# A transformer block on one core: the remainder of the expert weights formed by two engines, or by one

## The chip, the cores and the metric

The kernel runs on one core of one Trainium2 chip. The time is device microseconds (us) of one execution, the median of several. Lower is better. Five engines run side by side and meet only at semaphores: PE (TensorE, matrix products), DVE (VectorE), ACT (ScalarE), POOL (GpSimd) and SP (SyncE, which here only issues DMAs).

## The reference, cut to what matters

One layer: modulation, attention of two kinds, an output projection, and then a mixture of experts over 1024 tokens. Only the experts matter here, since the change lies wholly in them. Each token goes to 4 of 32 experts:

```
for each block of at most 128 tokens of one expert e:
    hu  = x @ w1[e] + b1[e]                       # 1024 -> 2048
    glu = min(hu[:, 0::2], 7); lin = clip(hu[:, 1::2], -7, 7)
    act = glu * sigmoid(1.702 * glu) * (lin + 1)  # 1024
    y   = act @ w2[e] + b2[e]                     # 1024 -> 1024
```

## The kernel before

The products are kept close to float32 by splitting both operands: a value is written as hi, its rounding to the fast float32 format (fp32r), and lo, the remainder. A product is then three passes: hi times hi, hi times lo of the weights, lo times hi.

**Steps.** A step is one expert with R = 1 or 2 blocks of 128 tokens. The loop of `program` runs a single step (R = 1) and then a double one (R = 2), over and over, and ends with single steps alone. In this run there are 35 steps: 16 pairs of a single and a double step, and 3 single steps at the end, so 19 single and 16 double ones.

**Units.** A step needs six weight units of 2 MB, each 128 partitions x 8 slices (k) x 512 columns: units 0 to 3 of w1 (`UP`), 4 and 5 of w2 (`DOWN`). For each unit and block PE does `product`: 8 slices x 3 passes = 24 matmuls. What happens to a unit n:
- SP loads it into a ring of three buffers, `ring[n % 3]` (L1163). The buffer becomes free when unit n - 3 has been split, so the load waits for `lo_done` (L1160, DVE's part) and `pool_lo_done` (L1161, POOL's part) of that unit.
- ACT writes `w_hi`, a ring of three, in two halves of four slices (L1256).
- The remainder `w_lo = ring - w_hi`, a ring of two, is formed by two engines. DVE does slices 0 to 3 in one instruction and slices 4 to 6 in a second (L1311). POOL does slice 7 (L1208).
- PE waits for each half before its first matmuls on it, and for POOL before slice 7.

**Order on each engine.** Every engine runs its list strictly in order.
- PE: products of units 0 to 3. After each one but the first come the transposes of the activations of the one before (L1389). Then, after unit 3, `rows(nxt, 0)`: it transposes the gathered tokens of the next step (L1382), which waits for the semaphore `gathered`, that is, for all gathers of the next step. Then unit 4, which waits at every second slice for `a_lo`, the lo part of the activations, and unit 5.
- DVE: when the products of unit n - 1 are done, the remainder of unit n + 1 (`split`). Then for each block of unit n the activation: `glu` (L1356), `lin` (L1357), their product (L1359), times the sigmoid of ACT (L1361), and `a_lo` (L1321) of the block before.
- POOL, besides slice 7 of each unit, carries the token traffic of the step. At the start of a step, when the outputs `y` of the step before are copied: `gate`, a tiny tensor operation (L1204), then R stores of y rows (L1239, an indirect DMA of 512 KB each), slice 7 of unit 1, a wait until the stores have landed, and in the next turn of its loop the row numbers (L1219), the load of the next step's token list (L1186), slice 7 of unit 2, a wait until that list has landed, a second `gate`, and the gathers of the next step's tokens (L1190, one indirect DMA of 512 KB for each block of the next step). A single step that is followed by a double one therefore gathers twice, and one that follows a double one stores twice.

The weight loads go through SP's DMA queue (q1), the stores, lists and gathers through POOL's (q0). Both end up on the same 16 DMA engines.

Of the kernel before, what the change touches and what calls it, by code (L numbers as in the profile page):

```python
# [17 lines left out]
F32 = mybir.dt.float32  # L18
# [4 lines left out]
ALU = mybir.AluOpType  # L23
# [5 lines left out]
KD = D // P  # L29
# [1053 lines left out]
def experts(K):  # L1083
# [4 lines left out]
    NU, RING, CH = UP + DOWN, 3, 2  # L1088
    HI, LO = 3, 2
    PAIRS = UNIT // 2  # L1090
    KC = KD // CH
    KP = KD - 1
    RMAX = 2
    ctx = ExitStack()
    with ctx:
        sb = lambda name, shape, dt=F32: ctx.enter_context(nc.sbuf_tensor(f"{name}_x", shape, dt))
        sem = lambda name: K.semaphores.enter_context(nc.semaphore(f"{name}_x"))
        ring = sb("wring", [P, RING, KD, UNIT])
        w_hi, w_lo = sb("w_hi", [P, HI, KD, UNIT], F32R), sb("w_lo", [P, LO, KD, UNIT], F32R)
# [11 lines left out]

        bias_loaded = sem("bias_loaded")
        w_loaded = [sem(f"w_loaded{r}") for r in range(RING)]
        hi_done, lo_done, pool_lo_done, prod_done = sem("hi_done"), sem("lo_done"), sem("pool_lo_done"), sem("prod_done")
        record_loaded, gathered, gate_open = sem("record_loaded"), sem("gathered"), sem("gate_open")
        xt_done, xhi_done, x_ready = sem("xt_done"), sem("xhi_done"), sem("x_ready")
        sel_up_ready, sel_down_ready = sem("sel_up_ready"), sem("sel_down_ready")
# [14 lines left out]
        def expert_of(engine, st):  # L1132
            steps_at = PAIR_AT if st.R == 2 else SINGLE_AT
            at = slice(steps_at, steps_at + 1) if isinstance(st.index, int) else bass.ds(st.index + steps_at, 1)
            return engine.value_load(K.table[0:1, at], min_val=0, max_val=E - 1)
# [4 lines left out]
        def units_done(st, units):  # L1140
            return NU * st.blocks + PROD0 + st.R * units
# [4 lines left out]
        def program(engine, body):  # L1146
            both, single = step_counts(engine)
            with engine.Fori(0, both) as b:
                body(Step(1, b, b), 2)
                body(Step(2, b + 1, b), 1)  # L1150
            with engine.Fori(both, single) as b:
                body(Step(1, b, both), 1)

        @block.sync
        def _(sp):
            def load(st, n, e):
                split_before = CH * (NU * st.passes + n) + CH
                if not isinstance(split_before, int):
                    split_before = sp.snap(split_before)
                sp.wait_ge(lo_done, split_before)  # L1160
                sp.wait_ge(pool_lo_done, split_before)  # L1161
                src = w1[bass.ds(e, 1), :, :, n * UNIT:(n + 1) * UNIT] if n < UP else w2[bass.ds(e, 1), :, :, (n - UP) * UNIT:(n - UP + 1) * UNIT]
                sp.dma_start(ring[:, n % RING, :, :], src.rearrange("a p k n -> (a p) k n")).then_inc(w_loaded[n % RING], 16)  # L1163

            first = Step(1, 0, 0)
            e_first = expert_of(sp, first)
            load(first, 0, e_first)
            sp.wait_ge(gathered, 16)
            load(first, 1, e_first)

            def body(st, next_r):
                nxt = st.then(next_r)
                e, e_next = expert_of(sp, st), expert_of(sp, nxt)
                for n in range(2, NU):
                    load(st, n, e)
                load(nxt, 0, e_next)
                load(nxt, 1, e_next)

            program(sp, body)

        @block.gpsimd
        def _(pool):
            def load_record(st):
                at = PAIR_AT if st.R == 2 else PAIR_SLOTS
                rows = slice(at, at + st.R * P) if isinstance(st.index, int) else bass.ds(st.index * (st.R * P) + at, st.R * P)
                pool.dma_start(record[:, 0:st.R, :], K.slot_d[rows, :].rearrange("(r p) a -> p r a", p=P)).then_inc(record_loaded, 16)  # L1186

            def gather(R):
                for r in range(R):
                    pool.indirect_dma_start(xg[:, r, :], None, K.h2_d, bass.IndirectOffsetOnAxis(ap=record[:, r, 0:1], axis=0)).then_inc(gathered, 16)  # L1190

            load_record(Step(1, 0, 0))
            pool.wait_ge(record_loaded, 16)
            gather(1)
            pool.sem_inc(y_free, 1)
            pool.memset(int_zero[:, :], 0).then_inc(gate_open, 1)
            pool.wait_ge(gate_open, 1)
            pool.memset(poolgate[:, :], 0.0).then_inc(gate_open, 1)
            pool.dma_start(onehot[:, :], io["k_onehot"]).then_inc(bias_loaded, 16)
            pool.dma_start(btab[:, :], K.btab_d).then_inc(bias_loaded, 16)  # L1200
            pool.wait_ge(gate_open, 2)

            def gate():
                pool.tensor_tensor(poolgate[:, 1:2], poolgate[:, 0:1], poolgate[:, 0:1], ALU.add).then_inc(gate_open, 1)  # L1204

            def split(unit, n):
                pool.wait_ge(hi_done, CH * unit + CH)
                pool.tensor_tensor(w_lo[:, n % LO, KP:, :], ring[:, n % RING, KP:, :], w_hi[:, n % HI, KP:, :].bitcast(F32), ALU.subtract).then_inc(pool_lo_done, CH)  # L1208

            pool.sem_inc(pool_lo_done, RING * CH)  # L1210
            pool.wait_ge(gathered, 16)
            split(0, 0)
            split(1, 1)

            def body(st, next_r):
                nxt = st.then(next_r)
                unit = NU * st.passes
                pool.wait_ge(gate_open, 3 * st.passes + 2)
                pool.tensor_tensor(y_row[:, 0:st.R], record[:, 0:st.R, 1], int_zero[:, 0:st.R], ALU.add).then_inc(gate_open, 1)  # L1219
                pool.wait_ge(gate_open, 3 * st.passes + 3)  # L1220
                load_record(nxt)
                pool.wait_ge(prod_done, units_done(st, 1))
                split(unit + 2, 2)
                pool.wait_ge(record_loaded, 16 * st.passes + 32)

                pool.wait_ge(xt_done, st.blocks + st.R)
                gate()
                gather(next_r)
                for n in range(3, NU):
                    pool.wait_ge(prod_done, units_done(st, n - 1))  # L1230
                    split(unit + n, n)
                pool.wait_ge(prod_done, units_done(st, NU - 1))
                split(unit + NU, 0)
                pool.wait_ge(gathered, 16 * (st.blocks + st.R + next_r))
                pool.wait_ge(gate_open, 3 * st.passes + 4)
                pool.wait_ge(y_copied, DOWN * (st.blocks + st.R) + 2)
                gate()
                for r in range(st.R):
                    pool.indirect_dma_start(K.y_d, bass.IndirectOffsetOnAxis(ap=y_row[:, r:r + 1], axis=0), y[:, r, :], None).then_inc(y_stored, 16)  # L1239
                pool.wait_ge(prod_done, units_done(st, NU))  # L1240
                split(unit + NU + 1, 1)
                pool.wait_ge(y_stored, 16 * (st.blocks + st.R))
                pool.sem_inc(y_free, 1)

            program(pool, body)
            pool.wait_ge(bias_loaded, 32)

# [54 lines left out]
        def _(dve):  # L1302
# [3 lines left out]

            def split(unit, n):
                for c in range(CH):
                    k = slice(KC * c, min(KC * (c + 1), KP))
                    dve.wait_ge(hi_done, CH * unit + c + 1)  # L1310
                    dve.tensor_tensor(w_lo[:, n % LO, k, :], ring[:, n % RING, k, :], w_hi[:, n % HI, k, :].bitcast(F32), ALU.subtract).then_inc(lo_done, 1)  # L1311

# [61 lines left out]
        def _(pe):  # L1374
# [17 lines left out]
            def product(st, n, r, bank, hi, lo, ready):  # L1392
                unit = NU * st.passes + n
                for c in range(CH):
                    if r == 0:
                        pe.wait_ge(lo_done, CH * unit + c + 1 + RING * CH)
                    for k in range(KC * c, KC * (c + 1)):
                        if r == 0 and k == KP:
                            pe.wait_ge(pool_lo_done, CH * unit + CH + RING * CH)
                        if ready:  # L1400
                            ready(k)
                        pe.matmul(bank, hi[:, r, k, :], w_hi[:, n % HI, k, :], start=False, stop=False)  # L1402
                        pe.matmul(bank, hi[:, r, k, :], w_lo[:, n % LO, k, :], start=False, stop=False)  # L1403
                        last = pe.matmul(bank, lo[:, r, k, :], w_hi[:, n % HI, k, :], start=False, stop=(k == KD - 1))  # L1404
                last.then_inc(prod_done, 1)
# [143 lines left out]
```

## Time and profile before

| what | value |
|---|---|
| median of 3 runs | 3359.65 us (3359.26 to 3365.08) |
| the profiled execution | 3360.82 us, its span 3359.2 us |
| busy share of the span: PE, DVE, ACT, POOL | 86%, 57%, 42%, 25% |
| TensorE clock granted, mean | 0.944 |
| expert stage | about 1262 to 3280 us of the span |
| POOL's remainder instructions, L1208 | 212 |

The span runs from the first to the last instruction. A busy share is an average over the whole span, and most of the span (some 2000 us) is the expert stage. The profile shows for every wait what ended it, and for every DMA the time from its issue to its landing.

### The profile page before, as it was taken

The numbers are of one execution on the slowest core, as the hardware profiler recorded it, in microseconds if no ns is written. First come the engines' busy times: TensorE is split into PE (matmuls) and PEld (weight loads), VectorE is DVE, ScalarE is ACT, GpSimd is POOL, SyncE is SP. The second block draws the span as 40 slices with busy tenths as digits, with TensorE's granted clock in tenths as the row PEclk, the third lists the DMA queues.
The fourth block names the chain that finished last, engine by engine and source line by source line (L and its number), as shares of the span: only waits on it lengthen the run. The fifth ranks groups of instructions, "written<-read, shape, count | busy, mean of one in ns | idle before, by whom it ended". The sixth has DMA issues, their size and how long they took to land. (4 is left out here: it accounts for less than half of the span.)

```text
span 3359.2 us, 40318 instructions
## 1 busy us (share of the span) xinstructions
PE 2876.1 (86%) x13206; PEld 2162.3 (64%) x13207; DVE 1903.3 (57%) x2864; ACT 1400.2 (42%) x1667; POOL 831.9 (25%) x609
## 2 busy tenths in 40 slices
PE   4899979998957707999999999999999999999980
PEld 0254667777734405777777777777777777777760
DVE  0430024454422256677767776866776687667786
ACT  0100125555521105445544554554455455545551
POOL 1000021212211143224322322332232233323340
PEclk8999989999978858999999999999999999999995
DMA  9700032323132108568657766775676577667678
GB/s 248 252 26 25 13 94 56 77 49 87 45 105 75 75 8 308 211 219 300 229 209 262 266 229 225 267 267 207 225 287 230 219 275 256 222 228 281 241 284 312
DMA packets 285165, 629.36 MB, mean 187 GB/s; under 512 B 9922, under 2 KB 11202, under 8 KB 284962
## 3 DMA queue, kind: packets, MB, share of 16 engines
q1 hardware_dynamic: 261558, 549.12, 47.7%
q0 software_dynamic: 23568, 79.73, 6.6%
q8 instruction: 23, 0.38, 0.0%
q14 instruction: 16, 0.13, 0.0%
HBM read 584.63 MB, written 50.26 MB: 189 GB/s over the span
## 5 line engine op out<-in xcount | busy, mean ns | idle before, releaser
L1311 DVE TENSOR_TENSOR w_lo_x<-wring_x,w_hi_x 128x2048 fp32r<-128x2048 f32 (+1 forms) x422 | 885.1, 2145 | 118.5 <-PE psum L1404 113.1
L1256 ACT ACTIVATE w_hi_x<-wring_x 128x2048 fp32r<-128x2048 f32 x424 | 787.8, 1909 | 148.9 <-DMA wring_x<-in_w_mlp 148.7
L1402 PE MATMUL psum<-w_hi_x,x_hi_x 128*128 128x512 f32 x1632 | 676.4, 414 | 8.5 <-DVE w_lo_x L1311 8.5
L1404 PE MATMUL psum<-w_hi_x,x_lo_x 128*128 128x512 f32 x1632 | 637.2, 390 | 0.0
L1403 PE MATMUL psum<-w_lo_x,x_hi_x 128*128 128x512 f32 x1632 | 637.0, 390 | 0.0
L1208 POOL TENSOR_TENSOR w_lo_x<-wring_x,w_hi_x 128x512 fp32r<-128x512 f32 x212 | 312.9, 1480 | 864.0 <-ACT w_hi_x L1256 464.6
L1402 PE MATMUL psum<-w_hi_x,a_hi_x 128*128 128x512 f32 x816 | 346.2, 424 | 51.9 <-DVE a_lo_x L1321 50.3
L1402 PEld LDWEIGHTS psum<-w_hi_x,x_hi_x 128*128 128x128 f32 x1632 | 308.4, 189 | 69.6 <-DVE w_lo_x L1311 10.6
L1404 PEld LDWEIGHTS psum<-w_hi_x,x_lo_x 128*128 128x128 f32 x1632 | 306.9, 188 | 65.9
L1403 PEld LDWEIGHTS psum<-w_lo_x,x_hi_x 128*128 128x128 f32 x1632 | 307.7, 189 | 62.2
L1403 PE MATMUL psum<-w_lo_x,a_hi_x 128*128 128x512 f32 x816 | 322.1, 395 | 0.0
L1404 PE MATMUL psum<-w_hi_x,a_lo_x 128*128 128x512 f32 x816 | 321.8, 394 | 0.0
L1286 ACT ACTIVATE sig_x<-glu_x 128x256 f32<-128x256 f32 x204 | 84.5, 414 | 478.0 <-DVE glu_x L1356 477.7
L1402 PEld LDWEIGHTS psum<-w_hi_x,a_hi_x 128*128 128x128 f32 x816 | 156.1, 191 | 98.5 <-DVE a_lo_x L1321 65.0
L1356 DVE TENSOR_SCALAR glu_x<-psum 128x256 f32<-128x256 f32 x204 | 85.2, 418 | 231.4 <-PE psum L1404 231.3
L654 ACT ACTIVATE S<-S,negm 128x896 f32<-128x896 f32 (+1 forms) x128 | 119.6, 935 | 208.1 <-DVE negm L717 113.5
L465 PE MATMUL psum<-hT,ring 128*128 128x512 f32 (+1 forms) x496 | 201.2, 565 | 5.0 <-DVE hT L381 4.4
L630 PE MATMUL psum<-v,PT 128*128 (+1 forms) x1536 | 187.0, 273 | 0.0
L630 PEld LDWEIGHTS psum<-v,PT 128*128 128x128 f32 x1536 | 183.6, 194 | 0.0
L1404 PEld LDWEIGHTS psum<-w_hi_x,a_lo_x 128*128 128x128 f32 x816 | 155.1, 190 | 34.3
L1403 PEld LDWEIGHTS psum<-w_lo_x,a_hi_x 128*128 128x128 f32 x816 | 156.1, 191 | 29.6
L1321 DVE TENSOR_TENSOR a_lo_x<-psum,a_hi_x 128x256 fp32r<-128x256 f32 x204 | 85.1, 417 | 149.8 <-ACT a_hi_x L1265 149.8
(249 smaller groups left out, 3535.6 us busy)
## 6 DMA issues: line engine op xcount, KB each, us to landing
wring_x<-in_w_mlp SPq DMA_DIRECT2D x212, 2048.0 KB, 8.2
ring<-in_w_ada SPq DMA_DIRECT2D x12, 2048.0 KB, 9.5
bias<-bias_d SPq DMA_DIRECT2D x16, 1280.0 KB, 14.2
yg<-y_d SPq DMA_DIRECT2D x8, 2048.0 KB, 10.4
ring<-in_w_in SPq DMA_DIRECT2D x4, 2048.0 KB, 9.6
xin<-in_x SPq DMA_DIRECT2D x8, 512.0 KB, 5.1
ring<-in_w_out SPq DMA_DIRECT2D x2, 2048.0 KB
mix_d<-o SPq DMA_DIRECT2D x8, 512.0 KB, 6.6
```

Source lines behind the costliest of these rows:

```text
L465: last = pe.matmul(ps[:, g % 4, 0:width], lhs, rhs, start=(k == 0), stop=(k == KD - 1))
L630: last = pe.matmul(ps[:, 6 + s // NHA, head * HD:(head + 1) * HD], PT[:, s % 2, c * P:(c + 1) * P], v, start=(c == 0), stop=(c == chunks - 1))
L654: act.activation(S[:, s % 2, 0:keys(s)], S[:, s % 2, 0:keys(s)], ACT.Exp, bias=negm[:, s:s + 1], accum_out=den[:, s:s + 1]).then_inc(p_don ...
L1208: pool.tensor_tensor(w_lo[:, n % LO, KP:, :], ring[:, n % RING, KP:, :], w_hi[:, n % HI, KP:, :].bitcast(F32), ALU.subtract).then_inc(pool ...
L1256: act.activation(w_hi[:, n % HI, k, :], ring[:, n % RING, k, :], ACT.Copy).then_inc(hi_done, 1)
L1286: act.activation(sig[:, j % 2, :], glu[:, j % 2, :], ACT.Sigmoid, scale=ALPHA).then_inc(sig_done, 1)
L1311: dve.tensor_tensor(w_lo[:, n % LO, k, :], ring[:, n % RING, k, :], w_hi[:, n % HI, k, :].bitcast(F32), ALU.subtract).then_inc(lo_done, 1)
L1321: dve.tensor_tensor(a_lo[:, r, 2 * n:2 * n + 2, :].rearrange("p k n -> p (k n)"), ps[:, 2 + j % 2, 0:2 * P], a_hi[:, r, 2 * n:2 * n + 2, : ...
L1356: dve.tensor_scalar(glu[:, s, :], pairs[:, :, 0], LIMIT, None, ALU.min).then_inc(glu_done, 1)
L1402: pe.matmul(bank, hi[:, r, k, :], w_hi[:, n % HI, k, :], start=False, stop=False)
L1403: pe.matmul(bank, hi[:, r, k, :], w_lo[:, n % LO, k, :], start=False, stop=False)
L1404: last = pe.matmul(bank, lo[:, r, k, :], w_hi[:, n % HI, k, :], start=False, stop=(k == KD - 1))
```

## The change

POOL no longer takes part in the remainder. DVE's second instruction of each unit covers slices 4 to 7 instead of 4 to 6. The semaphore `pool_lo_done` and the waits for it, in SP's load and before PE's slice 7, are gone, and so are POOL's waits for products and for `hi_done`.

```
-                sp.wait_ge(pool_lo_done, split_before)
...
-            def split(unit, n):
-                pool.wait_ge(hi_done, CH * unit + CH)
-                pool.tensor_tensor(w_lo[:, n % LO, KP:, :], ring[:, n % RING, KP:, :], w_hi[:, n % HI, KP:, :].bitcast(F32), ALU.subtract).then_inc(pool_lo_done, CH)
...
                 load_record(nxt)
-                pool.wait_ge(prod_done, units_done(st, 1))
-                split(unit + 2, 2)
                 pool.wait_ge(record_loaded, 16 * st.passes + 32)
...
                 gather(next_r)
-                for n in range(3, NU):
-                    pool.wait_ge(prod_done, units_done(st, n - 1))
-                    split(unit + n, n)
-                pool.wait_ge(prod_done, units_done(st, NU - 1))
-                split(unit + NU, 0)
...
-                pool.wait_ge(prod_done, units_done(st, NU))
-                split(unit + NU + 1, 1)
                 pool.wait_ge(y_stored, 16 * (st.blocks + st.R))
...
             def split(unit, n):
                 for c in range(CH):
-                    k = slice(KC * c, min(KC * (c + 1), KP))
+                    k = slice(KC * c, KC * (c + 1))
                     dve.wait_ge(hi_done, CH * unit + c + 1)
...
-                        if r == 0 and k == KP:
-                            pe.wait_ge(pool_lo_done, CH * unit + CH + RING * CH)
```

## Rows read from the trace of the kernel before

**Rows 1.** Who waited for whom, 1100 to 3300 us: total, times, longest.
```profile
PE psum L1382 <- DMA xg_x<-h_d,record_x: 104.9, 18, 81.9
PE psum L1402 <- DVE a_lo_x L1321: 50.3, 49, 1.7
...
PE psum L1402 <- DVE w_lo_x L1311: 9.9, 9, 6.4
```

**Rows 2.** Groups of instructions on DVE, shapes kept apart, 1050 to 3300 us.
```profile
L1311 DVE TENSOR_TENSOR w_lo_x<-wring_x,w_hi_x 128x2048 fp32r<-128x2048 f32 x211 | 520.8, 2468 | 118.5 <-PE psum L1404 113.1 <-ACT w_hi_x L1256 5.4
L1311 DVE TENSOR_TENSOR w_lo_x<-wring_x,w_hi_x 128x1536 fp32r<-128x1536 f32 x211 | 384.3, 1821 | 0.0
```

**Rows 3.** POOL's timeline at the start of the stage: the first gather, after its list.
```profile
1264.25 1.01 POOL L1190 DMA_INDIRECT xg_x<-h_d,record_x  x1 [1.65 <-DMA record_x<-slot_d]
```

**Rows 4.** DVE's timeline of a single step: start, us, instruction, idle before.
```profile
1402.82 3.96 DVE L1311 TENSOR_TENSOR w_lo_x<-wring_x,w_hi_x 128x2048 fp32r<-128x2048 f32 x2 [8.21 <-PE psum L1404]
...
1422.75 3.28 DVE L1361 TENSOR_TENSOR act_o_x<-lin_x,sig_x 128x256 f32<-128x256 f32 x1 [0.61 <-ACT sig_x L1286]
...
1426.29 5.04 DVE L1311 TENSOR_TENSOR w_lo_x<-wring_x,w_hi_x 128x2048 fp32r<-128x2048 f32 x2
1431.25 0.41 DVE L1356 TENSOR_SCALAR glu_x<-psum 128x256 f32<-128x256 f32 x1
...
1433.16 0.21 DVE L1327 CAST sel_up_x<-onehot_x 96x128 bf16 x1
```

**Rows 5.** POOL's timeline of the same step.
```profile
1407.96 0.97 POOL L1239 DMA_INDIRECT y_d<-y_x,y_row_x  x1 [0.30 <-issue]
1408.94 1.31 POOL L1208 TENSOR_TENSOR w_lo_x<-wring_x,w_hi_x 128x512 fp32r<-128x512 f32 x1
...
1413.95 0.78 POOL L1186 DMA_DIRECT2D record_x<-slot_d  x1 [0.70 <-POOL y_row_x L1219]
...
1418.91 0.48 POOL L1204 TENSOR_TENSOR poolgate_x<-poolgate_x 128x1 f32<-128x1 f32 x1 [2.85 <-DMA record_x<-slot_d]
1419.60 2.30 POOL L1190 DMA_INDIRECT xg_x<-h_d,record_x  x1 [0.21 <-issue]
1422.21 0.96 POOL L1190 DMA_INDIRECT xg_x<-h_d,record_x  x1 [0.30 <-issue]
1423.18 2.55 POOL L1208 TENSOR_TENSOR w_lo_x<-wring_x,w_hi_x 128x512 fp32r<-128x512 f32 x2
```

**Rows 6.** PE's timeline of the same step.
```profile
1427.29 1.09 PE L1382 MATMUL psum<-ident,xg_x 128*128 128x128 f32 x8 [0.77 <-DMA xg_x<-h_d,record_x]
...
1433.30 0.50 PE L1402 MATMUL psum<-w_hi_x,a_hi_x 128*128 128x512 f32 x1 [1.66 <-DVE a_lo_x L1321]
...
1436.12 0.50 PE L1402 MATMUL psum<-w_hi_x,a_hi_x 128*128 128x512 f32 x1 [0.93 <-DVE a_lo_x L1321]
```

**Rows 7.** SP's DMA queue: what its loads waited for, 1300 to 3200 us.
```profile
SPq L1161 <- POOL w_lo_x L1208: 912.8, 180, 15.0
```

**Rows 8.** Weight loads in SP's timeline: two of the single step, one of a double step.
```profile
1410.47 0.37 SPq L1163 DMA_DIRECT2D wring_x<-in_w_mlp  x1
...
1424.70 0.37 SPq L1163 DMA_DIRECT2D wring_x<-in_w_mlp  x1
...
1328.31 0.37 SPq L1163 DMA_DIRECT2D wring_x<-in_w_mlp  x1
```

**Rows 9.** The two y stores of the single step, from issue to landing.
```profile
DMA to landing us min/median/max: 3.5/4.1/4.7
```

**Rows 10.** The two gathers of the single step, from issue to landing.
```profile
DMA to landing us min/median/max: 5.0/5.4/5.8
```

**Rows 11.** DMA issues of a double step, 1319 to 1355 us: count, size, median to landing.
```profile
y_d<-y_x,y_row_x POOLq DMA_INDIRECT x1, 9.6
...
xg_x<-h_d,record_x POOLq DMA_INDIRECT x1, 8.1
```

**Rows 12.** A stretch after a wait of PE: busy, clock granted, DMA.
```profile
1390.00:1393.50 3.50, 3.50 (x10) 2.76 (x9) 3.50 (x2) 3.49 (x2) 0.79 (x1) 0.52 0.69 198
```

More of the change, by code:

```diff
@@ L1091, in experts @@
     KC = KD // CH
-    KP = KD - 1
     RMAX = 2
@@ L1113, in experts @@
         w_loaded = [sem(f"w_loaded{r}") for r in range(RING)]
-        hi_done, lo_done, pool_lo_done, prod_done = sem("hi_done"), sem("lo_done"), sem("pool_lo_done"), sem("prod_done")
+        hi_done, lo_done, prod_done = sem("hi_done"), sem("lo_done"), sem("prod_done")
         record_loaded, gathered, gate_open = sem("record_loaded"), sem("gathered"), sem("gate_open")
@@ L1204, in gate @@
                 pool.tensor_tensor(poolgate[:, 1:2], poolgate[:, 0:1], poolgate[:, 0:1], ALU.add).then_inc(gate_open, 1)
-            def split(unit, n):
-                pool.wait_ge(hi_done, CH * unit + CH)
-                pool.tensor_tensor(w_lo[:, n % LO, KP:, :], ring[:, n % RING, KP:, :], w_hi[:, n % HI, KP:, :].bitcast(F32), ALU.subtract).then_inc(pool_lo_done, CH)
-            pool.sem_inc(pool_lo_done, RING * CH)
             pool.wait_ge(gathered, 16)
-            split(0, 0)
-            split(1, 1)
             def body(st, next_r):
                 nxt = st.then(next_r)
-                unit = NU * st.passes
                 pool.wait_ge(gate_open, 3 * st.passes + 2)
```

## The prediction

> **What bounds the kernel now.** I read four views: who waited for whom, the groups of instructions, the timelines of one single step on each engine, and the DMAs' times from issue to landing. The reader should see that PE is the bound almost everywhere, and that its few waits sit in the single steps. In the expert stage PE waits for the tokens of the next step (104.9 us, of which 81.9 are the one wait before the stage; 23.0 remain), for `a_lo` (50.3 us in 49 waits) and hardly for the weights' remainder (9.9 us, of which 6.4 is the first unit) [rows 1]. In double steps PE works twice as long on each weight unit, and everything else has room. So the single steps decide, 19 of them, and I follow the one that starts at 1402.5 us.
>
> DVE runs without a pause in it and is held up by POOL. A pair of remainder instructions takes 3.96 us there when nothing interferes, and 5.04 us later in the same step; a multiplication that touches 256 columns takes 3.28 us at 1422.75 [rows 4]. That one ends just after POOL's two remainders, back to back from 1423.18 for 2.55 us [rows 5]. So instructions of the two engines that read SBUF exclude each other. PE pays 1.66 us at 1433.30 for the late `a_lo`; its next wait, 0.93 us, is the way PE-ACT-DVE of the last block and stays [rows 6].
>
> The other wait of the single step is the gather: PE stands 0.77 us before L1382, at 1427.29 [rows 6]. The gathers were issued at 1419.60 and 1422.21 [rows 5] and landed 5.0 us after the second issue [rows 10]. This chain has no slack, and what the change does to it decides.
>
> **The change, part by part.** *DVE's work.* One eighth more: 3.96 us x 512/3584 = 0.57 us a unit, so a pair takes 4.5 us; 212 units make 120 us of DVE time. From below, the mean of the pair now is 2.47 + 1.82 = 4.29 us [rows 2], 0.33 over the free pair, and that excess goes: the net per pair is 0.24 us. The short instructions gain besides. Does it reach PE? After the first block's activation, about 1410.5, DVE has three pairs (13.5 us) and three blocks of activation at 1.91 us each (1431.25 to 1433.16 [rows 4]): 1410.5 + 13.5 + 5.7 = 1429.7. PE wants that `a_lo` at 1431.6 (its start less its wait). So 1.9 us are left, DVE's extra work is hidden behind PE's products, and the wait of 1.66 us goes. Over all steps: 50.3 us less 35 x 0.93 = 17.7 us, and 9.9 - 6.4 = 3.5 us for the first steps. The gain is **-21 us**. If the cover were gone, 3 x 0.57 = 1.7 us a single step would show.
>
> *POOL's work.* 212 instructions go, all off the path. None of them delays a gather today: the stores end at 1408.93, the remainder fits in before they land; the next fits in before the list lands [rows 5].
>
> *The loads.* This is where I expect the price. SP waited 912.8 us in 180 waits for POOL's part of the remainder, last of all [rows 7]. In the single step POOL finishes unit 1 at 1410.25, since its stores come first, and the load follows at 1410.47 [rows 5, 8]; DVE had finished at 1406.78. With the wait gone the load goes out at 1402.82 + 4.5 + 0.1 = 1407.4, that is 3.1 us earlier and before the second y store (1407.96). The load of unit 0 of the next step goes out at about 1421.5 in place of 1424.70 [rows 8], so before the gathers have landed, and the one after it at about 1427.9. Today stores and gathers of the single steps fall in holes that POOL's late remainder makes.
>
> What such a hole is worth: alone, a store lands 3.5 us after its issue [rows 9]. In a double step a store issued within 0.1 us of a load (1328.31 [rows 8]) lands after 9.6 us, and a gather of 512 KB after 8.1 us, where the single step's two together need 5.0 after the second issue [rows 10, 11]. So I have a store or gather behind a load wait for that load.
>
> Step by step. The second store lands at 1407.4 + 9.6 = 1417.0 at most, 1411.5 at least as now; I take 1416.5, near the upper end, since its load is ahead of it: +5.0. The list of tokens was issued 2.4 us after that landing (1413.95) and lands 1.1 us before the gather chain goes on; it is issued at about 1418, behind the load of unit 5 (1415), and lands at 1423 instead of 1418.8: +4.3. The second gate reads SBUF and meets DVE's pair for unit 4 (from 1423.3), whose half takes 2.2 us: between 0 and 2.2 us more. The gathers are issued as now, 3.3 us after the gate's end, and land 5.0 us after the second issue [rows 10] if they find a hole, 8.1 [rows 11] if not: between 0 and 3.1 us more. In all the gathers land between 4.1 and 9.5 us later. I take 5.7, in the lower half, because the upper ends need both collisions. 16 single steps that end in two gathers or follow two stores: 16 x 5.7 = **+91 us** (66 to 152). The last two single steps store and gather once, and their stores already stood behind a load: +2 us together. The first has no store before it: 0.
>
> *The clock.* After waits of PE in a double step the granted clock was 0.52 for 3.5 us, the lower level of 1.2 GHz [rows 12], and those matmuls took 1.6 us longer in all. A wait of six or seven us may bring the same: 0 to 1.6 us a single step, 0 to 26 us; I take **+10**, as today only a few waits bring it.
>
> Sum: 3360.8 - 21 + 91 + 2 + 10 = 3443 us for a profiled execution. The median of the runs was 1.2 us below the profiled one, so about **3441 us**, 2.4% slower.
>
> **The rivals.** *1. The transfers share, and the gathers come no later.* Stores and gathers take turns with a load instead of waiting for it. The two gathers land at 1425.4 and 1427.2 (issues and 5.8 and 5.0 us [rows 5, 10]), so one transfer of 512 KB takes 1.8 us of the DMA engines; at half pace the store and the last gather lose up to 1.8 us each. But the list of tokens, 1 KB, would then pass a load. Now it costs 0.78 + 1.30 + 2.85 = 4.9 us from issue to the end of POOL's wait [rows 5]; at the start of the stage, with nothing else under way, POOL stood only 1.65 us for it after the issue [rows 3], so some 2.6 us come back. In sum -2.6 to +1.0 us; at 0 only the gain is left: 3360 - 21 = **3339 us**. For it: nothing in the kernel orders the two queues. Against it: the 9.6 and 8.1 us [rows 11], which are 5 to 6 us and 3 us more than in a hole, not 1.8. The Trainium skill (DMA: Bandwidth & Descriptors, Queues, rings and completion order) says that each DMA engine goes round between the queues that have work for it and switches after every packet, which speaks for this rival and, by its time, for a faster kernel; the trace agrees only if a packet is long.
>
> *2. DVE becomes the bound.* If POOL's remainders are not what makes the long instructions [rows 4], nothing is given back and every single step is 1.7 us longer: 19 x 1.7 = 32, **3392 us**. It decides from the point where DVE's chain is 1.9 us later than I have it. Against it: the long ones lie exactly beside POOL's remainders [rows 4, 5].
>
> *3. Nothing reaches PE.* Gain and price cancel: the gathers land 1.3 us later only (21/16). **3360 us**. Nothing singles this value out.
>
> **How the numbers follow.** Late gathers 0.70, rival 1 0.18, rival 2 0.06, rival 3 0.06. A measurement of this kernel tells 0.2%, 6.7 us. The forecast is 3441 us. Its own range is 3385 (16 x 4.1, no clock) to 3512 (16 x 9.5 and 26 of clock). The range over all cases runs from 3338, the middle of rival 1, to 3490; the part of the late gathers above 3490 is small, as it needs every bound at its worst. Faster 0.19, same 0.07, slower 0.74.
>
> **What would show it.** In the changed kernel's single steps: the first load at about 5 us after the step's start instead of 8; the second y store 8 to 9 us from issue to landing instead of 3.5; the gathers issued 5 to 7 us later; PE's wait before L1382 at 100 us and more in the stage instead of 23; its waits for `a_lo` down to about 33 us; no DVE pair above 4.6 us except beside a gate; double steps as long as before. I would be wrong if stores and loads share the DMA engines packet by packet, or if something I read as cause, the hole, only happens to lie there.

## The result

The changed kernel takes 3529.9 us (median, 3523.1 to 3539.1) against 3360.9 us: ratio 1.0503, 95% interval 1.0476 to 1.0529. That is 169 us slower. I had forecast 3441 us and a range up to 3490: the right direction and half the size.

Who waited for whom on PE in the changed kernel, 1100 to 3480 us (its L1363 and L1381 are L1382 and L1402 of before):

```profile
PE psum L1363 <- DMA xg_x<-h_d,record_x: 281.6, 19, 85.2
...
PE psum L1381 <- DVE a_lo_x L1302: 32.6, 35, 0.9
...
PE psum L1381 <- DVE w_lo_x L1292: 6.2, 6, 1.9
```

Against [rows 1]: the wait for the gathered tokens, less the one ahead of the stage, went from 23.0 to 196.4 us, in 18 of the 19 single steps (all but the first). The waits for `a_lo` fell from 50.3 to 32.6 us, which is 35 times the 0.93 us that I had left standing. So PE lost 173 us at one place and gained 21 us at others.

The group of DVE's remainders shows that the two engines no longer exclude each other: one mean, 2284 ns for 2048 columns, where [rows 2] has 2468.

```profile
L1292 DVE TENSOR_TENSOR w_lo_x<-wring_x,w_hi_x 128x2048 fp32r<-128x2048 f32 x422 | 943.3, 2284 | 114.8 <-PE psum L1383 113.6 <-ACT w_hi_x L1237 1.2
```

Now the same single step as in [rows 5], which starts at 1399.8 us here. POOL's timeline:

```profile
1402.68 2.85 POOL L1222 DMA_INDIRECT y_d<-y_x,y_row_x  x1 [0.17 <-issue]
1405.83 0.98 POOL L1222 DMA_INDIRECT y_d<-y_x,y_row_x  x1 [0.30 <-issue]
1415.71 0.78 POOL L1209 TENSOR_TENSOR y_row_x<-record_x,int_zero_x 128x1 int32<-128x1 int32 x1 [8.90 <-DMA y_d<-y_x,y_row_x]
...
1423.68 2.88 POOL L1188 DMA_INDIRECT xg_x<-h_d,record_x  x1 [0.16 <-issue]
1426.86 0.95 POOL L1188 DMA_INDIRECT xg_x<-h_d,record_x  x1 [0.30 <-issue]
```

DVE's pair for this stretch, SP's loads, and PE:

```profile
1400.16 4.50 DVE L1292 TENSOR_TENSOR w_lo_x<-wring_x,w_hi_x 128x2048 fp32r<-128x2048 f32 x2 [8.23 <-PE psum L1383]
```

```profile
1404.83 0.37 SPq L1161 DMA_DIRECT2D wring_x<-in_w_mlp  x1
...
1418.82 0.37 SPq L1161 DMA_DIRECT2D wring_x<-in_w_mlp  x1
```

```profile
1434.87 1.97 PE L1363 MATMUL psum<-ident,xg_x 128*128 128x128 f32 x8 [11.45 <-DMA xg_x<-h_d,record_x]
```

The two y stores of this step, then its two gathers, from issue to landing:

```profile
DMA to landing us min/median/max: 8.9/9.5/10.1
```

```profile
DMA to landing us min/median/max: 8.0/8.5/9.1
```

The first load goes out 5.0 us after the step's start in place of 8.0, before either store is fully issued: DVE's pair ends at 1404.66, the load follows 0.17 us later, and the first store's instruction ends 0.87 us after the pair, at 1405.53. The stores take 10.1 us (the first) and 8.9 us to land where they took 4.7 and 3.5 [rows 9]. Unit 0 of the next step goes out at 1418.82, and the gathers take 8.0 us and more where they took 5.0 [rows 10]. PE stands still for 11.45 us at 1434.87. The median of the 15 single steps between double ones went from 41.65 to 51.87 us, the double ones stayed at 74.27 us.

What the DMA engines did with the load of 1404.83 and the two stores stands in the packets of the two queues: first 1404.8 to 1409 us, with the load's time to landing, then 1410.5 to 1413.5 us (packets, MB, share):

```profile
q1 hardware_dynamic: 340, 0.70, 66.6%
...
wring_x<-in_w_mlp SPq DMA_DIRECT2D x1, 2048.0 KB, 11.5
```

```profile
q0 software_dynamic: 211, 0.80, 64.9%
q1 hardware_dynamic: 213, 0.44, 37.3%
```

So the stores don't wait for the load's end. They start late: up to 1409 us only the load's queue (q1) moves anything. Then the two queues take turns, 211 packets against 213, and both stores have landed, at 1412.8 and 1414.7, before the load does at 1416.3. In the medians of the 15 steps the first store's first packet comes 4.2 us after the end of its issue (0.6 before the change), and its data then takes 2.4 us (1.45 before). Most of the delay is the late start, about 1 us is the sharing.

The clock granted while PE waits, and after, 1428 to 1434 and 1435 to 1439 us (busy PE, PEld, DVE, ACT, POOL; clock; DMA share; GB/s):

```profile
1428.00:1434.00 6.00, 0.00 (x0) 0.00 (x0) 0.00 (x0) 0.00 (x0) 0.00 (x0) 0.50 1.03 401
1435.00:1439.00 4.00, 4.00 (x14) 3.48 (x15) 1.07 (x1) 1.02 (x1) 0.00 (x0) 0.50 0.13 48
```

In PE's long wait the clock is at the lower level, and PE's first 4 us after it run at 1.2 GHz. From 1300 us to the end of the stage the lower level holds for 236 us in all against 24 before; for 140 of the 236 us PE stands still anyway.

### The profile page after: what moved, and what is told of

It is laid out like the page before. It is cut to its first block and busy times, and to the rows that moved or that the text cites. A ratio compares the mean times of both kernels' runs of the same rounds, so it can differ in the third digit from the quotient of the medians.

```text
span 3537.5 us, 39263 instructions
## 1 busy us (share of the span) xinstructions
PE 2902.8 (82%) x13206; PEld 2193.8 (62%) x13207; DVE 1845.0 (52%) x2864; ACT 1401.6 (40%) x1667; POOL 533.5 (15%) x397
## 5 line engine op out<-in xcount | busy, mean ns | idle before, releaser
L1292 DVE TENSOR_TENSOR w_lo_x<-wring_x,w_hi_x 128x2048 fp32r<-128x2048 f32 x422 | 943.3, 2284 | 114.8 <-PE psum L1383 113.6
L1381 PE MATMUL psum<-w_hi_x,x_hi_x 128*128 128x512 f32 x1632 | 676.7, 415 | 5.3 <-DVE w_lo_x L1292 5.3
L1382 PE MATMUL psum<-w_lo_x,x_hi_x 128*128 128x512 f32 x1632 | 637.4, 391 | 0.0
L1381 PE MATMUL psum<-w_hi_x,a_hi_x 128*128 128x512 f32 x816 | 356.0, 436 | 33.6 <-DVE a_lo_x L1302 32.6
L1381 PEld LDWEIGHTS psum<-w_hi_x,x_hi_x 128*128 128x128 f32 x1632 | 308.5, 189 | 66.2 <-DVE w_lo_x L1292 7.0
L1382 PEld LDWEIGHTS psum<-w_lo_x,x_hi_x 128*128 128x128 f32 x1632 | 307.8, 189 | 62.1
L1382 PE MATMUL psum<-w_lo_x,a_hi_x 128*128 128x512 f32 x816 | 328.7, 403 | 0.0
L1202 POOL TENSOR_TENSOR poolgate_x<-poolgate_x 128x1 f32<-128x1 f32 x70 | 83.7, 1196 | 1533.1 <-ACT y_x L1276 1386.0
L1363 PE MATMUL psum<-ident,xg_x 128*128 128x128 f32 x416 | 71.6, 329 | 281.6 <-DMA xg_x<-h_d,record_x 281.6
L1363 PEld LDWEIGHTS psum<-ident,xg_x 128*128 128x128 f32 x416 | 60.1, 171 | 288.1 <-DMA xg_x<-h_d,record_x 286.0
L1381 PEld LDWEIGHTS psum<-w_hi_x,a_hi_x 128*128 128x128 f32 x816 | 161.8, 198 | 74.0 <-DVE a_lo_x L1302 40.9
```

The source lines that it names most:

```text
L1363: last = pe.transpose(ps[:, 6 + k // 4, (k % 4) * P:(k % 4 + 1) * P], xg[:, r, k * P:(k + 1) * P], K.ident[:, :])
```

## The experiments

Ratios are to the kernel before. "After" names the changed kernel (1.0503). "PE's wait for the gathers" is always the total less the one wait of 82 to 86 us ahead of the stage: 23.0 us before, 196.4 after.

### Holding back one load or both, for the transfers

The first kernel holds the load of unit 4 until the stores of the step before have landed (the call that passes `hold=True` is left out here):

```
 def load(st, n, e, hold=False):
+    if n == UP and hold:
+        free = sp.snap(st.passes + 1)
+        sp.wait_ge(y_free, free)
     sp.wait_ge(lo_done, split_before)
```

> The changed kernel with one wait more on SP: the load of unit 4 (the third load of a step) waits until the y stores of the step before have landed. Theory of the holes: the stores land about 3.5 us after their issue again instead of 9.9, the rest of the chain still meets loads, so about half of the loss comes back: 3380 to 3440 us. If the loss is in the gathers' own collision alone: above 3500 us.

Measured 3430.4 us, ratio 1.0213 (1.0191 to 1.0236). More than half of the loss is back. The stores of one of its single steps land nearly as they did before the change (3.5 and 4.7 us):

```profile
DMA to landing us min/median/max: 3.5/4.4/5.2
```

The second holds the load of the next step's unit 0 until the gathers have landed:

```
+    sp.wait_ge(gathered, sp.snap(16 * (st.blocks + st.R + next_r)))
     load(nxt, 0, e_next)
```

> The changed kernel with another wait on SP: the load of the next step's unit 0 waits until the gathers for that step have landed. Theory of the holes: the gathers land 5.0 us after the second issue instead of 7.9, everything before them is as late as in the changed kernel: about 3 us for each of 18 single steps, 3460 to 3490 us. If the stores and the list are the whole loss: 3520 us or more.

Measured 3493.5 us, ratio 1.0386 (1.0368 to 1.0403): 3 us above the expected range. PE starts on the gathered tokens 32.4 us after the step's start instead of 35.3 (medians), so the 3 us are there; the double steps got slightly longer.

Both together:

> The changed kernel with both waits on SP: the load of unit 4 waits for the y stores to land, the load of the next step's unit 0 for the gathers. Theory of the holes: the two gains add up to nearly all of the loss, except that the token list still meets a load: 3370 to 3410 us. If they don't add up: above 3420 us.

Measured 3387.9 us, ratio 1.0085 (1.0068 to 1.0102), in the range. But the single steps are now 40.6 us, better than before the change, and the double ones 77.2 us. Hence the same holds in single steps alone (`if st.R == 1` on both):

> The changed kernel with both loads held for the stores and the gathers, but in the single steps alone. With the holds in all steps the single steps came down to 40.6 us, below the 41.65 us of the kernel before, and the double ones rose to 77.2 from 74.3 us. Theory: the double steps return to 74.3 us and the single ones stay: 3387 - 38 = about 3350 us, 3340 to 3362. If the hold of one single step works through into the double one after it: 3370 us or more.

Measured 3389.9 us, ratio 1.0088 (1.0073 to 1.0102). The main expectation failed and its alternative, 3370 us or more, came true: the double steps stay at 76.4 us. PE's waits for `w_lo` in the stage are 27.0 us (6.2 after), most of them of about 2 us at the start of double steps: the unit 0 that was held back in the single step comes late for the double one. What the holds give to the tokens they take in part from the weights.

### The turn without the work, and the work without the turn

GpSimd waits for the same semaphores at the same places as before, and only counts; the loads wait for its count:

```
+def turn(unit, n):
+    pool.wait_ge(hi_done, CH * unit + CH)
+    pool.sem_inc(pool_turn, CH)
...
 sp.wait_ge(lo_done, split_before)
+sp.wait_ge(pool_turn, split_before)
```

> The changed kernel, with DVE forming the whole remainder, but GpSimd still takes its turn at each unit: it waits for the same semaphores at the same places as in the kernel before, and then only counts up, without subtracting; the loads wait for that count again. Theory of the holes (stores, token list and gathers wait behind weight loads that now go out earlier): the time falls to about that of the kernel before or below it, 3310 to 3345 us, since DVE's extra work is covered and the two engines no longer exclude each other; PE's wait for the gathers in the stage falls from about 196 us to 10 to 35 us. Rival, DVE's longer work is the cost: 3390 us or more. Rival, the missing work of GpSimd itself changes the order of things: stays near 3530 us.

Measured 3477.9 us, ratio 1.0351 (1.0329 to 1.0374): far from the range of the holes. By its number alone it would fit the rival of DVE's longer work, 3390 us or more, but the timeline shows that the kernel is not the one that I had meant. In the single step that starts at 1898.2, POOL's second store and SP's first load:

```profile
1904.17 0.97 POOL L1238 DMA_INDIRECT y_d<-y_x,y_row_x  x1 [0.30 <-issue]
```

```profile
1903.17 0.37 SPq L1162 DMA_DIRECT2D wring_x<-in_w_mlp  x1
```

The bare count was made before the second store, which stands ahead of it in POOL's program, had even started, and the load went out after 5.0 us as in the changed kernel. It was no undoing of the change. So the turn was made an instruction of the engine:

```
-    pool.sem_inc(pool_turn, CH)
+    pool.memset(turnbox[:, n:n + 1], 0.0).then_inc(pool_turn, CH)
```

> As the kernel where GpSimd only takes its turn, but the turn is now a small instruction of the engine itself (a memset of one column), which queues up behind the y stores and the gathers as the subtraction did; the bare count of the run before was made 2 us before the stores had been worked off. Theory of the holes: the first load of the single step goes out at about 7 us after the step's start instead of 5, and the load of the next unit 0 after the gathers; the stores land about 3.5 us after their issue and the time is 3310 to 3350 us. Rival, DVE's longer work costs what that kernel had lost: it stays above 3390 us.

Measured 3396.3 us, ratio 1.0105 (1.0088 to 1.0122). In the step that starts at 1870.1 the load goes out at 1877.37, after both stores, and they land in 4.4 and 5.2 us:

```profile
1877.37 0.37 SPq L1163 DMA_DIRECT2D wring_x<-in_w_mlp  x1
```

```profile
DMA to landing us min/median/max: 4.4/4.8/5.2
```

134 us of the 169 are back, and DVE does the whole remainder as in the changed kernel; only the order of GpSimd and the loads is the old one. That is the main reading. But the time misses the range that the theory gave by 46 us and lies in that of the rival, DVE's longer work (above 3390 us), so something else costs too. With the turn as a subtraction of the old length, on data of its own:

```
+    pool.tensor_tensor(spare[:, 2, :], spare[:, 0, :], spare[:, 1, :], ALU.subtract).then_inc(pool_turn, CH)
```

> As the kernel with the turn on the engine, but the turn is a subtraction of 128x512 on data of its own, as long as the one before. This is the kernel before with its order and exclusion, plus DVE's longer second instruction. Theory of the holes: 3360 to 3390 us, since all transfers fall where they did, and DVE is at most 3 x 0.57 us later in each single step. Rival, DVE as the bound: 3390 to 3420 us. The difference to the run with the memset prices the exclusion of the two engines.

Measured 3389.9 us, ratio 1.0093 (1.0080 to 1.0106), on the border between the theory's range and the rival's. This is close to the kernel before but for DVE's longer instruction (besides, PE no longer waits for GpSimd's part, and GpSimd waits for its own subtraction), and it costs 33 us. PE's wait for the gathers is 46.6 us, twice that of before: 24 of the 33 us. And the counterpart, the same subtraction without any load waiting for it:

> The changed kernel, but GpSimd does at each unit a subtraction of the same size as before (128x512), on data of its own that nobody reads, at the same places; the loads don't wait for it. Theory of the holes: the time stays at that of the changed kernel or above it, 3525 to 3580 us, because the work covers nothing and excludes DVE as before. Rival, it was GpSimd's work or the exclusion that gave the single steps their timing: near 3360 us.

Measured 3571.9 us, ratio 1.0622 (1.0604 to 1.0640). GpSimd's work is no cover; what mattered was that loads waited for it.

### Shorter pieces on DVE

In the kernel before, the first gather of the pair took 2.30 us to issue [rows 5], and it takes 2.88 us now, the first store 2.85. Is that DVE's instruction, 0.5 us longer? The rows say so: POOL's instruction ends 0.87 us after DVE's pair in both kernels, at 1407.65 (the first store, 1405.32 and 2.33 us) after a pair from 1402.82 to 1406.78 [rows 4] and at 1405.53 after one from 1400.16 to 1404.66, and the pair ends 0.5 us later in its step. Now DVE's remainder in four instructions instead of two, first in the changed kernel:

```
-dve.tensor_tensor(w_lo[:, n % LO, k, :], ...).then_inc(lo_done, 1)
+for h in range(2):
+    q = slice(KC * c + 2 * h, KC * c + 2 * h + 2)
+    ins = dve.tensor_tensor(w_lo[:, n % LO, q, :], ring[:, n % RING, q, :], w_hi[:, n % HI, q, :].bitcast(F32), ALU.subtract)
+ins.then_inc(lo_done, 1)
```

> The changed kernel, with DVE's remainder of a unit in four instructions of 1024 columns instead of two of 2048. The same work, but GpSimd's gate, its row numbers and the issue of its indirect DMAs find a gap after at most 1.2 us instead of 2.3 us. Theory of the exclusion as a part of the loss: the gate and the first indirect DMA end 1 to 2 us earlier, the gathers land about 1 to 3 us earlier in each single step: 3480 to 3515 us. If only the loads' timing matters: within 8 us of the changed kernel.

Measured 3488.6 us, ratio 1.0370 (1.0342 to 1.0397). The pieces are worth 41 us in the changed kernel. POOL's stores in the step that starts at 1891.7, and their landing:

```profile
1893.46 1.80 POOL L1222 DMA_INDIRECT y_d<-y_x,y_row_x  x1 [0.15 <-issue]
1895.57 1.94 POOL L1222 DMA_INDIRECT y_d<-y_x,y_row_x  x1 [0.31 <-issue]
```

```profile
DMA to landing us min/median/max: 4.1/6.5/8.9
```

```profile
1896.84 0.37 SPq L1161 DMA_DIRECT2D wring_x<-in_w_mlp  x1
```

This is the cleanest picture of the two queues. The first store is issued by 1895.26, before the load, and lands in 4.1 us; the second is done at 1897.51, 0.7 us after the load's issue, and takes 8.9 us. It too lands ahead of that load, at 1904.4 against 1906.8. In the changed kernel the first store too was done only at 1405.53, after the load at 1404.83, and so both were late.

Then in the kernel that has the old order and DVE's longer work:

> The kernel where GpSimd takes its turn with a subtraction as long as before, on data of its own, and DVE's remainder of a unit is in four instructions of 1024 columns. That kernel without the pieces was about 33 us slower than the kernel before, with the order of all transfers kept. Theory: DVE's longer second instruction keeps GpSimd's gate and the issue of its indirect DMAs waiting for 0.5 to 1.5 us more in each single step; with short pieces this goes: 3340 to 3370 us. Rival, it is DVE's own length on PE's path: 3385 us or more.

Measured 3410.1 us, ratio 1.0138 (1.0122 to 1.0155): the time went the wrong way, into the rival's range (3385 us or more). PE's wait for the gathers is down to 6.7 us from 46.6, which fits a GpSimd that DVE's long instructions had kept waiting. In its place the waits for `a_lo` and `w_lo` rose from 41.9 and 16.1 to 73.9 and 21.8 us. So the pieces gave the gathers back but not the time: once the gathers are in time, PE waits for the activations and the weights.

### The token list ahead of the stores' landing

The list is loaded right behind the issue of the stores, with two places for the row numbers, first without any turn (the edit in part: the wait for the stores' landing moves behind the list's load):

```
...
 load_record(nxt)
+pool.wait_ge(y_stored, 16 * st.blocks + 16)
+pool.sem_inc(y_free, 1)
```

> The changed kernel with only the token list loaded early, right behind the issue of the y stores and without waiting for their landing; the loads go out as in the changed kernel. Theory of the chain: the list no longer waits for the stores behind a load, it is issued 9 us earlier in the single step, so most of the 10 us by which the gathers are late come back: 3370 to 3430 us. If the gathers' own collision with the loads is what counts: above 3480 us.

Measured 3424.0 us, ratio 1.0170 (1.0154 to 1.0186): 106 of the 169 us go with the list alone, though every load goes out as in the changed kernel. So most of the loss goes through the chain in which the list has to wait for late stores; the gathers' own wait is still 79.6 us in the stage. With the turn on the engine as well:

> As the kernel with the turn on the engine, and the token list of the next step is loaded right behind the issue of the y stores, before the turn that lets the next weight load go, instead of after the stores' landing; y_row has one place for single and one for double steps. Theory of the holes: the list lands 3 to 5 us earlier, the gathers are issued at 13 to 16 us after the step's start instead of 17, and PE's wait for them nearly ends: 3290 to 3320 us. If the gathers then meet the load that was sent before them, they land as late as before: within 10 us of the run with the turn on the engine.

Measured 3370.7 us, ratio 1.0033 (1.0021 to 1.0046): between the two expected ranges, 26 us better than with the turn alone. PE no longer waits for a gather in the stage, but for `a_lo`:

```profile
PE psum L1384 <- DMA xg_x<-h_d,record_x: 81.9, 1, 81.9
...
PE psum L1402 <- DVE a_lo_x L1323: 73.6, 53, 2.7
```

The load of unit 5 now meets the gathers: in the single step that was followed before, it is issued 12.7 us after the start and lands after 12.1 us, where it took 7.7 before the change. ACT waits 3.8 us for it, and the last sigmoid stands behind. Three attempts to go on from there or to bring the same to the kernel before:

> The kernel with the early token list and the turn on the engine, and ACT does the last sigmoid of a step before the high part of unit 5, not after it. In the run with the early list PE no longer waits for the gathers but for the activations, which wait for this sigmoid, which stands behind the high part of unit 5, which waits for its load. Theory: the single step falls from 40.8 to about 38.5 us, 3320 to 3345 us. If another thing is late by then, for example DVE: within 10 us of the run with the early list, 3370 us.

Measured 3400.7 us, ratio 1.0112 (1.0095 to 1.0129). Failed: the waits for `a_lo` rose to 90.7 us. Perhaps the high part of unit 5, moved behind the sigmoid, holds up what follows on ACT; that was not followed up.

> The kernel before (GpSimd still subtracts its eighth and the loads wait for it) with only the token list loaded early, right behind the issue of the y stores. Theory: the gathers are issued 3 to 6 us earlier, PE's 23 us of waiting for them in the stage go, but DVE is still held up by GpSimd's subtractions and the loads may come later: 3330 to 3360 us.

Measured 3444.0 us, ratio 1.0245 (1.0224 to 1.0266). Failed, and plainly: the gathers no longer keep PE waiting, but the loads go out later (9.7 us after the step's start), and the waits are 82.7 us for `a_lo` and 29.1 for `w_lo`.

> The kernel with the early token list and the turn on the engine, with DVE's remainder in four instructions. The gathers had already stopped keeping PE waiting there; the load of unit 5 was late instead. Theory: the stores and gathers go out 1 to 2 us earlier and leave the DMA engines to the loads earlier: 3345 to 3370 us. If DVE's extra instructions cost more than that: 3375 us or more.

Measured 3369.2 us, ratio 1.0027 (1.0017 to 1.0037), in the range: single steps 40.5 us, double ones 76.0 (medians). Of the 16 double steps nine take 76 us, and in each of these the clock stands at the lower level for 3.4 us; the others take 74.4. This is the best kernel with DVE's whole remainder, and still not faster than the one before. Last, the pieces with both holds in the single steps:

> The same with DVE's remainder in four instructions, which shortens the wait of GpSimd's gate and indirect DMAs. In the changed kernel the pieces brought the gathers 3.7 us earlier; here PE's wait for them is about 2.6 us in a single step, so at most 18 x 2.6 us are to be had: 3310 to 3345 us. If the pieces only move the wait elsewhere: within 8 us of the run without them.

Measured 3394.0 us, ratio 1.0097 (1.0083 to 1.0112). Failed as a gain, and within 8 us of the run without pieces, the alternative: single steps 39.9 us, double ones 78.8.

## Why the prediction had the direction right and the size wrong

*The gain, -21 us.* Right. The waits for `a_lo` and `w_lo` fell by 17.7 and 3.7 us.

*DVE's extra work hidden.* Right for PE's path in the changed kernel: its `a_lo` came in time, 27.4 us after the step's start. But I had looked only at PE as the one who waits for DVE.

*The loads go out earlier, and the token traffic that meets them is late.* Right, and shown from both sides: loads held back by a turn (134 us back), stores alone protected (99 us back), the list taken out of the chain (106 us back), work without a turn (nothing back).

*A store or gather behind a load waits for that load.* Right in its times, 8.9 and 10.1 us against the 9.6 of the sum, and wrong as a mechanism. The store starts late, then shares, and lands before the load: in each of the 15 single steps both stores and both gathers landed 1.0 to 4.0 us ahead of the load issued just before them. Why the first packet comes so late is not shown. That it is due to the load is: with the load held back the stores take 3.5 and 5.2 us.

*The size of +91 us: the step that failed.* I took the gathers to come 5.7 us later, "in the lower half, because the upper ends need both collisions", with bounds of 4.1 and 9.5. They came 10.1 us later (median of 15 single steps: PE starts on them 35.3 instead of 25.2 us after the step's start). By parts, before to after, in the same medians: end of the second store's issue +0.6; from there to the row numbers 3.1 to 8.6, +5.5; row numbers to list -0.2; list to gate +0.3; gate to the end of the gathers' issue 4.5 to 5.6, +1.1; from there to PE 4.5 to 7.3, +2.8. In my sum the gathers' own collision could be 0 to 3.1 and the gate's 0 to 2.2. Both collisions were there in every one of these steps: it was a matter of order, not of chance, and the order could have been read off. The next unit 0's load at 1421.5 of my own sum lay ahead of gathers that I had issued after 1423. And "the gathers are issued as now" was wrong: DVE's longer instruction holds up POOL's first indirect DMA of a pair (2.30 to 2.88 us). With all loads in the old order the longer instruction costs 33 us, 24 of them in the wait for the gathers; in the changed kernel shorter pieces take back 41. The sum also saw only the second store behind the load. The first one's instruction ends 0.87 us after DVE's pair and the load goes out 0.17 us after it, so the first store falls behind as well. Last, the range of the late gathers was added up wrongly: with 16 x 4.1 and no clock it begins at 3359.6 - 21 + 66 + 2 = about 3406 us and not at 3385, and its upper end is about 3519 and not 3512. The measured time lies above either.

*The single steps at the end, +2 us.* Too small: the last two of those that are timed in full went from 39.8 and 41.2 to 50.7 and 47.8 us. Their stores stood behind a load already, but list and gathers did not.

*The clock, +10 us.* Mis-sized. The ledger of the profiled executions is 178.3 us of span: +173.4 gathers, -21 the other waits; the remaining 26 us are near my upper end (0 to 26). Before, unit 4's products ran at the lower level in few single steps, now in nearly all. The remainder agrees with what PE itself did: its 8466 matmuls of the stage kept it busy for 1898.1 us against 1872.2, 26 us longer, and the lower level held for 96 us of its busy time against 24. No experiment separates the clock from another cause of longer matmuls.

*Rival 1, the transfers share.* Its mechanism is there, its time is refuted. The Trainium skill (DMA: Bandwidth & Descriptors, Queues, rings and completion order) says that an engine goes round between its queues after each packet. The trace agrees: once the stores had started, 211 packets of their queue went against 213 of the loads' in 3 us, with packets of 4 KB and 2 KB, so no long packet is needed for it. The sharing costs about 1 us a store, within the rival's 1.8. What the rival had at nothing is the late start: 4.2 us in place of 0.6.

*Rival 2, DVE as the bound.* Wrong for the changed kernel, but it is what stands next: where the gathers were put right, PE waited for `a_lo`.

*What stays open.* What holds back the first packet of a store or gather whose load was issued just before. No version with DVE's whole remainder beat the kernel before; the best was 0.3% slower. Whether the rest is the clock after PE's waits or the loads' order in the step wasn't separated.

## What to carry to other kernels

A wait that looks redundant can be what keeps two streams of transfers apart. Before taking one away, list every DMA that it delayed, and put the new issue times into one list with the other queue's: here a 512 KB transfer whose issue ended 0.7 to 3 us after that of a 2 MB one moved its first packet only 3 to 5 us later and landed after 7 to 11 us in place of 3.5 to 6, though it still landed first in the single steps. Where a chain has several links that each go through the DMA engines, and the order at each link is fixed, add up all collisions rather than half of them.

And look in both directions for an instruction that grows: not only who waits for its result, but also which engine can't start while it runs.

## What the runs showed of the hardware

- A store of 512 KB whose issue ends before a 2 MB load's lands in 4.1 us; one that ends 0.7 us after it takes 8.9 us, on another queue.
- The late store doesn't wait for the load's end: its first packet comes 4.2 us after its issue (0.6 without a load), then the queues take turns (211 packets against 213 in 3 us), and the two stores land 1.5 to 3.6 us before the load.
- GpSimd's indirect DMA instruction is held up by DVE's subtraction with two SBUF inputs: the first of two took 2.33 us beside a DVE pair of 3.96 us and 2.85 beside one of 4.50, in both cases ending 0.87 us after the pair. With DVE's pieces half as long the two took 1.80 and 1.94 us.
- A semaphore count in GpSimd's program didn't wait for the indirect DMAs ahead of it: the load that waited for it went out at 5.0 us, and with a memset in its place at 7.3 us.
- A wait of PE of 11.45 us brought the granted clock to 0.50 during the wait, and PE's next 4 us of matmuls ran at it.
